# Mixer of block 1: weights rounded first in each step, attention outputs copied out of PSUM, statistic and gate rows and the second output turn later

## The reference

```python
h = rmsnorm(x, mix_norm_pre[l])
z = h @ w_in[l]
aq, ak, av, mq, mk, mv, mo, mi, mf, gl = jnp.split(z, SPLIT_IDX, axis=-1)
ya = diff_attention(aq, ak, av, lam, lam_init, attn_norm_w[l])   # 8 heads
mqk = jax.nn.silu(causal_depthwise_conv(jnp.concatenate([mq, mk], axis=-1), conv_w[l], conv_b[l]))
hm = mlstm_chunkwise(...mqk..., mv, mi + igate_b[l], mf + fgate_b[l])
ym = (jax.nn.sigmoid(mo) * rmsnorm(hm, mlstm_norm_w[l]).reshape(b_, s_, M_V))
g_a, g_m = jnp.split(jax.nn.sigmoid(gl + gate_b[l]), 2, axis=-1)
merged = g_a * (ya @ w_proj_a[l]) + g_m * (ym @ w_proj_m[l])
x = x + rmsnorm(merged @ w_out[l], mix_norm_post[l])
```

## Time and profile before

| | us |
|---|---|
| Runs, median (lowest to highest of 3) | 2140.96 (2139.83 to 2142.47) |
| The profiled execution | 2136.9 |
| Its span, first to last instruction | 2135.1 |
| TensorE busy | 2005.8 |
| VectorE busy | 1342.9 |
| ScalarE busy | 1077.9 |
| Mean granted TensorE clock, share of full | 0.973 |

### The profile page before, as it was taken

The page is one execution under the profiler, slowest core; times in us unless marked ns, Lnnn a source line. Parts: engine busy times, 40 slices in busy tenths (PEclk is TensorE's granted clock), DMA queues, the critical chain, the costliest instruction groups (busy, mean ns, idle before and its releaser), DMA issues. The chain is left out here.

```text
span 2135.1 us, 31214 instructions
## 1 busy us (share of the span) xinstructions
PE 2005.8 (94%) x12360; PEld 1768.7 (83%) x12360; DVE 1342.9 (63%) x2263; ACT 1077.9 (50%) x1669; POOL 228.1 (11%) x212
## 2 busy tenths in 40 slices
PE   7999978999999999989799999997989998999997
PEld 5887778899788778878789978876889997789997
DVE  6555667466755565566756675557578865668874
ACT  5445456564544554455564554444355545346553
POOL 1000301000100000011100010002104400303420
PEclk9999999999999999999999999997999999899998
DMA  7554434535555365544354455553235563334552
GB/s 255 188 188 156 139 101 143 169 126 183 191 191 188 120 215 188 188 138 129 103 184 135 155 188 189 190 168 102 86 118 188 180 216 117 99 119 154 182 194 73
DMA packets 92737, 338.30 MB, mean 158 GB/s; under 512 B 10288, under 2 KB 10544, under 8 KB 92592
## 3 DMA queue, kind: packets, MB, share of 16 engines
q1 hardware_dynamic: 91296, 330.69, 46.6%
q0 software_dynamic: 720, 4.69, 0.6%
q10 hardware_dynamic: 576, 0.92, 0.1%
HBM read 335.21 MB, written 1.05 MB: 157 GB/s over the span
## 5 line engine op out<-in xcount | busy, mean ns | idle before, releaser
L983 DVE TENSOR_TENSOR w_lo<-w_raw,w_hi 128x1024 fp32r<-128x1024 f32 x628 | 790.1, 1263 | 479.6 <-ACT w_hi L534 477.4
L534 ACT ACTIVATE w_hi<-w_raw 128x1024 fp32r<-128x1024 f32 x628 | 658.9, 1054 | 432.3 <-PE stream L1746 197.1
L1738 PE MATMUL stream<-h_hi,w_hi 128*128 128x256 f32 x1632 | 480.7, 295 | 12.1 <-DVE h_lo L1357 9.6
L1739 PE MATMUL stream<-h_lo,w_hi 128*128 128x256 f32 x1632 | 467.5, 286 | 0.0
L1740 PE MATMUL stream<-h_hi,w_lo 128*128 128x256 f32 x1632 | 467.3, 286 | 0.0
L1738 PEld LDWEIGHTS stream<-h_hi,w_hi 128*128 128x128 f32 x1632 | 317.1, 194 | 25.4 <-issue 18.1
L1744 PE MATMUL stream<-w_hi,h_hi 128*128 128x512 f32 x800 | 314.6, 393 | 6.1 <-DVE h_lo L996 6.1
L1739 PEld LDWEIGHTS stream<-h_lo,w_hi 128*128 128x128 f32 x1632 | 318.1, 195 | 0.2
L1740 PEld LDWEIGHTS stream<-h_hi,w_lo 128*128 128x128 f32 x1632 | 317.7, 195 | 0.0
L1746 PE MATMUL stream<-w_lo,h_hi 128*128 128x512 f32 x800 | 313.1, 391 | 0.0
L1745 PE MATMUL stream<-w_hi,h_lo 128*128 128x512 f32 x800 | 312.9, 391 | 0.0
(11 more groups left out here) (309 smaller groups left out, 2981.0 us busy)
## 6 DMA issues: line engine op xcount, KB each, us to landing
w_raw<-in_w_up SPq DMA_DIRECT2D x264, 512.0 KB, 3.5
w_raw<-in_w_mix SPq DMA_DIRECT2D x228, 512.0 KB, 3.5
w_raw<-in_w_down SPq DMA_DIRECT2D x136, 512.0 KB, 3.5
params<-in_params POOLq DMA_DIRECT2D x4, 921.5 KB, 5.2
out_x<-x_residual SPq DMA_DIRECT2D x4, 256.0 KB, 2.3
constants<-in_consts POOLq DMA_DIRECT2D x1, 896.0 KB, 7.8
x_residual<-in_x ACTq DMA_DIRECT2D x3, 256.0 KB, 4.1
x_residual<-in_x SPq DMA_DIRECT2D x1, 256.0 KB, 3.9
```

The costliest lines, as they stand in the source:

```text
L534: nc.scalar.activation(w_hi[:, u % RING], w_raw[:, u % RAW], ACT.Copy).then_inc(hi_ready, 1)
L983: nc.vector.tensor_tensor(w_lo[:, u % RING], w_raw[:, u % RAW], w_hi[:, u % RING].bitcast(F32), ALU.subtract).then_inc(split_done, 1)
L1738: nc.tensor.matmul(dst, w_hi[:, s, w], hi, start=first, stop=False)
L1739: nc.tensor.matmul(dst, w_hi[:, s, w], lo, start=False, stop=False)
```

## The change

- In each step, ScalarE calls `hi_next()` first; before, it stood behind the exponentials, the transposed weights' copy, the squares and the roundings of the outputs. Eight roundings and splits instead of five stand ahead of the statistics, and none between the v copies.
- `o_square` becomes `o_take`: ScalarE copies both PSUM tiles into `o_n` (SBUF) and squares from there. The values of head 4, and the first mLSTM values that reuse the tiles, wait for these copies; `o_scale` works on `o_n` in place. The wait for the turns that still read `o_n` goes from VectorE to ScalarE.
- Statistic rows move from within unit 5 to step 8, gate rows from within unit 6 to step 10; the ScalarE and VectorE work on them moves to steps 10 and 11, the maxima to steps 16 to 23, the split of the rows to step 25.
- The second pair of output turns moves from steps 32, 33 to 35, 37 on all three engines; on ScalarE `ya_round` now stands ahead of the exponentials of its step.
- The sigmoids of `gl` start at step 65.

```diff
@@ -447,6 +447,7 @@
         tok_bank = ((bank[0], bank[1]), (side[0], side[1]), (bank[2], bank[0]), (bank[1], bank[2]),
                     (bank[0], bank[1]), (bank[2], bank[0]))
         GROUPS = ((0, 3), (3, 6), (6, 8))
+        YA_TURN = (25, 27, 35, 37)
         YM_TURN = (57, 63, 65, 68)
 
         def out_bank(i):
@@ -667,10 +668,15 @@
                         act.wait_ge(o_ready, n8 + h)
                     nc.scalar.activation(aT[:], bank[3][:, 0:3 * P], ACT.Copy).then_inc(aT_stored, 1)
 
-                def o_square(b):
+                def o_take(b):
                     act.wait_ge(o_ready, n8 + 4 * b + 4)
+                    if b > 0:
+                        act.wait_ge(ya_turned, l * 4 + 2)
                     for t in range(QT):
-                        nc.scalar.activation(o_sq[:, t], side[2 + t][:], ACT.Square).then_inc(o_squared, 1)
+                        nc.scalar.activation(o_n[:, t], side[2 + t][:], ACT.Copy).then_inc(o_squared, 1)
+                    for t in range(QT):
+                        act.wait_ge(o_squared, (l * 2 + b) * 4 + 2)
+                        nc.scalar.activation(o_sq[:, t], o_n[:, t], ACT.Square).then_inc(o_squared, 1)
 
                 def o_rstds(b):
                     act.wait_ge(o_stat, (l * 2 + b) * 5 + 4)
@@ -725,7 +731,7 @@
                         nc.scalar.activation(yms_hi[:, 2 * p + j], bank[3][:, j * T:(j + 1) * T], ACT.Identity,
                                              scale=p1("mlstm_norm", 2 * p + j)).then_inc(ym_hi_done, 1)
 
-                for j in range(5):
+                for j in range(8):
                     hi_next()
                 act.wait_ge(pre_stat, n + 1)
                 nc.scalar.activation(ln_all[:], bank[3][:, 0:T + QT], ACT.Ln, bias=eps1[:]).then_inc(pre_ln, 1)
@@ -733,25 +739,24 @@
                 nc.scalar.activation(rs_all[:], ln_all[:], ACT.Exp, scale=-0.5).then_inc(pre_rs, 1)
                 act.wait_ge(pre_rs, n + 1)
                 store(0, lambda t: av_tok[:, t, 0:512])
-                hi_next()
-                hi_next()
-                lam_exponents()
-                hi_next()
                 store(1, lambda t: av_tok[:, t, 512:D])
                 for i in range(U_QK, U_OUT):
-                    if i == U_QK + 1:
+                    hi_next()
+                    if i == U_QK + 2:
+                        lam_exponents()
+                    if i == U_QK + 3:
                         gates()
+                    if i in YA_TURN:
+                        k = YA_TURN.index(i)
+                        ya_round(k // 2, k % 2)
                     if i % 2 and 11 <= i <= 25:
                         attn_exp((i - 11) // 2)
                     if i % 2 == 0 and 14 <= i <= 28:
                         attn_turned((i - 14) // 2)
                     if i in (21, 29):
-                        o_square((i - 21) // 8)
+                        o_take((i - 21) // 8)
                     if i in (22, 30):
                         o_rstds((i - 22) // 8)
-                    if i in (25, 27, 32, 33):
-                        k = (25, 27, 32, 33).index(i)
-                        ya_round(k // 2, k % 2)
                     if i == 34:
                         nc.scalar.preload_act_table_set("silu_and_others")
                         act.wait_ge(conv_done, (l + 1) * 8)
@@ -791,8 +795,8 @@
                             mlstm_rstd(g)
                     if i in YM_TURN:
                         ym_round(YM_TURN.index(i))
-                    if 66 <= i < 70:
-                        for m in range(4 * (i - 66), 4 * (i - 65)):
+                    if 65 <= i < 69:
+                        for m in range(4 * (i - 65), 4 * (i - 64)):
                             act.wait_ge(gl_scaled, l * 16 + m + 1)
                             nc.scalar.activation(gl[:, m], gl[:, m], ACT.Sigmoid,
                                                  bias=p1("gate_b", m)).then_inc(gl_sig, 1)
@@ -1174,7 +1178,7 @@
                     k = (l * 2 + b) * 5
                     dve.wait_ge(p_ready, n8 + 4 * b + 4)
                     nc.vector.reciprocal(o_r0[:], aden[:, 4 * b:4 * b + 4, 0:2])
-                    dve.wait_ge(o_squared, (l * 2 + b) * 2 + 2)
+                    dve.wait_ge(o_squared, (l * 2 + b) * 4 + 4)
                     for t in range(QT):
                         nc.vector.tensor_reduce(o_var[:, :, t], o_sq[:, t].rearrange("p (h d) -> p h d", h=4), AX.X,
                                                 ALU.add).then_inc(o_stat, 1)
@@ -1188,11 +1192,9 @@
                     dve.wait_ge(o_rstd, l * 2 + b + 1)
                     nc.vector.tensor_tensor(o_r0[:], o_r0[:], o_rs[:], ALU.mult).then_inc(o_stat, 1)
                     dve.wait_ge(o_stat, k + 5)
-                    if b > 0:
-                        dve.wait_ge(ya_turned, l * 4 + 2)
                     for t in range(QT):
                         nc.vector.tensor_tensor(o_n[:, t].rearrange("p (h d) -> p h d", h=4),
-                                                side[2 + t][:].rearrange("p (h d) -> p h d", h=4),
+                                                o_n[:, t].rearrange("p (h d) -> p h d", h=4),
                                                 o_r0[:, :, t].unsqueeze(2).to_broadcast([P, 4, P]),
                                                 ALU.mult).then_inc(o_scaled, 1)
 
@@ -1284,29 +1286,27 @@
                                                 ALU.subtract).then_inc(mix_lo, 1)
 
                 prepare()
-                for j in range(5):
+                for j in range(8):
                     lo_next()
                 dve.wait_ge(pre_rs, n + 1)
                 scales()
-                lo_next()
-                lo_next()
-                rows()
-                lo_next()
                 for i in range(U_QK, U_OUT):
+                    if i == U_QK + 2:
+                        rows()
                     if i % 2 and 11 <= i <= 25:
                         attn_mask((i - 11) // 2)
                     if i % 2 == 0 and 12 <= i <= 26:
                         attn_combine((i - 12) // 2)
                     if i in (22, 30):
                         o_stats((i - 22) // 8)
-                    if 14 <= i < 22:
-                        gate_max(i - 14)
-                    if i == 23:
+                    if 16 <= i < 24:
+                        gate_max(i - 16)
+                    if i == 25:
                         split_rows()
                     if i == 31:
                         g_tok()
-                    if i in (25, 27, 32, 33):
-                        k = (25, 27, 32, 33).index(i)
+                    if i in YA_TURN:
+                        k = YA_TURN.index(i)
                         ya_rest(k // 2, k % 2)
                     lo_next()
                     if i in (22, 30):
@@ -1945,7 +1945,7 @@
                 def values(h):
                     pe.wait_ge(aT_stored, n8 + h + 1)
                     if h == 4:
-                        pe.wait_ge(o_scaled, l * 4 + 2)
+                        pe.wait_ge(o_squared, l * 8 + 2)
                     v, c = av_tok[:, :, h * P:(h + 1) * P], blk(h % 4)
                     nc.tensor.matmul(side[2][:, c], aT[:, 0:P], v[:, 0], start=True, stop=True)
                     nc.tensor.matmul(side[3][:, c], aT[:, P:T], v[:, 0], start=True, stop=False)
@@ -1988,7 +1988,7 @@
                             if g == 0:
                                 pe.wait_ge(tok_stored, l * 12 + 12)
                                 pe.wait_ge(nm_cleared, l + 1)
-                                pe.wait_ge(o_scaled, l * 4 + 4)
+                                pe.wait_ge(o_squared, l * 8 + 6)
                             else:
                                 pe.wait_ge(num_taken, (l * 3 + g) * 2)
                             first = a
@@ -2049,21 +2049,21 @@
                         chunk(0, j, t)
                 for j in range(4):
                     unit(u0 + 4 + j)
-                    chunk(1, j, 0)
-                    if j == 1:
+                    for t in range(QT):
+                        chunk(1, j, t)
+                for i in range(U_QK, U_OUT):
+                    if i == U_QK:
                         stat_rows()
-                    chunk(1, j, 1)
-                    if j == 2:
+                    if i == U_QK + 2:
                         gates()
-                for i in range(U_QK, U_OUT):
                     if i % 2 and 11 <= i <= 25:
                         scores((i - 11) // 2)
                     if i % 2 == 0 and 14 <= i <= 28:
                         turn_a((i - 14) // 2)
                     if i % 2 and 15 <= i <= 29:
                         values((i - 15) // 2)
-                    if i in (25, 27, 32, 33):
-                        k = (25, 27, 32, 33).index(i)
+                    if i in YA_TURN:
+                        k = YA_TURN.index(i)
                         ya_turn(k // 2, k % 2)
                     if i == 31:
                         g_tok()
```

## The result

| | before | after |
|---|---|---|
| Runs beside each other, median us (lowest to highest, 4 each) | 2141.72 (2139.83 to 2142.92) | 2085.93 (2084.01 to 2088.39) |
| The profiled execution, us | 2136.9 | 2084.01 |
| Its span, us | 2135.1 | 2082.2 |
| Mean granted TensorE clock | 0.973 | 0.979 |

The ratio is 0.9741, 95% interval 0.9724 to 0.9758: 55.8 us less, 2.6%. The forecast was 2097, so 44 us less, and its range began at 2091; the time lies 5 us under it. The direction was right, and the waits that were to go are gone, but for a rest of 1.0 us. The size was 9 us of span too small, and the prices that the single parts were given did not hold, as the experiments show.

A forecast was written before the change was run, and what follows sets the result against it. TensorE, busy 94%, was taken as the bound, leaving only its stalls and half clock: 41.1 us of waits plus 6.95 for clock is 48.0, less 4 is 44.0, so 2140.96 falls to 2097 us; 8-in-10 range 2091 to 2108.

The forecast's parts named there:

- Weights first: Attention steps of both mixers: rounding ahead of the exponentials makes k copies timely, ending score waits of 9.0 + 3.6 = 12.6 us.
- Outputs leave PSUM at once: Fifth head's values, both mixers: they wait only for two ScalarE copies, not the scaled outputs; 12.1 us gained, added costs taken as 0.
- Statistic rows later: Start of both mixers: rows moved behind more token units no longer wait for GpSimd's sum; 4.4 us gained.
- Second turn later, ya_lo and the merge: Later mixer steps: waits for gate columns (6.8 us), ya_lo (3.8 us) and the gated merge (1.4 us) go.
- The half clock: Four stretches behind stalls in the mixers: 13.9 us of TensorE work at clock 0.50 takes twice as long, costing 6.95 us.
- What comes late next: Steps 22 to 33: VectorE falls 4.0 us behind per layer, split lead absorbs part; 2 us per layer allowed, 4 us off.
- the ceiling of 48.0 us: Both mixers of block 1: all winnable time, 41.1 us of waits plus 6.95 for the clock; set the range's lower end.
- VectorE as the bound (2105): Rival, steps 22 to 33: VectorE's 4.0 us lag per layer is not absorbed; gain 36.0 us, 2105 us; 18%.
- the q copy (2109.5): Rival, attention scores: they wait for ScalarE's q copy, not k, so 12.6 us stay; gain 31.4, 2109.5 us; 8%.
- the slower case (2215): Rival, steps 8 to 63: rounding first delays ScalarE results TensorE needs at once, 1.05 us each, 118 us, 2215 us; 3%.

The follow-up runs named there:

- the experiment with the k copy: Kernel before, with VectorE's k copy ahead of the split in odd steps and ScalarE untouched: 2132.41 us against 2134.16, ratio 0.9988.
- the loaded kernel: Kernel after, with VectorE repeating its split in six steps of each mixer, 12 extra splits: 2100.78 us against 2133.9 for the kernel before, ratio 0.9834.

## Why the prediction was right, and where its size was off

**Weights first**, 12.6 us: right in mechanism. The split follows the maxima, the k copy is in time, and the chain ends at k and not q, as the experiment with the k copy shows. The gain in this stretch is 13.4. But as a price of the part 12.6 is far too low: alone it gives 31 us. The single terms were attached to the wrong owners. That their sum still comes near is luck of a kind: all parts were made together, so it didn't matter which of them a wait belonged to.

**Outputs leave PSUM at once**, 12.1 us: 12.3 measured with the other parts there. Alone it loses 6 us, and taken out it costs only 7, wait and clock together. The costs that I set to 0 by their cover, in the tile view (duration min/median/max, ns):

```profile
L676 ACT ACTIVATE o_normed<-acc x8: 572/582/602, 290.6 to 1007.7; 128x512 f32<-128x512 f32 x8
L679 ACT ACTIVATE o_squares<-o_normed x8: 614/624/634, 291.6 to 1008.9; 128x512 f32<-128x512 f32 x8
```

The copies take 0.58 us (0.6 assumed), the squares from SBUF 0.62 and so 0.10 more than from PSUM, the upper end of my 0 to 0.8 us in all. The second scaling runs beside GpSimd:

```profile
326.62 1.85 DVE L1196 TENSOR_TENSOR o_normed<-o_normed,o_row_scales 128x512 f32<-128x512 f32 x2
```

The first one, in the timeline above, took 1.29 us, this one 1.85: 0.56 more a layer, near the upper end of 0.7. Of its two instructions the first takes the usual 0.69 us and the second 1.24. GpSimd's own instruction beside it is longer as well, 1.14 us against 0.77 for the same one 4.6 us earlier:

```profile
322.14 0.77 POOL L1628 TENSOR_TENSOR conv_in<-conv_raw,mix_rstd 128x256 f32<-128x256 f32 x1 [3.12 <-ACT conv_raw L782]
326.79 1.14 POOL L1628 TENSOR_TENSOR conv_in<-conv_raw,mix_rstd 128x256 f32<-128x256 f32 x1 [3.87 <-ACT conv_raw L782]
```

So the engine that comes second loses each time, as the rule of the Trainium skill, SBUF — State Buffer, section "SBUF: two separate sides", would have it: GpSimd's instruction starts 0.17 us into the first scaling and is stretched, and the second scaling starts inside it and is stretched in turn. The size is about that of the convolution rows. Both costs are real, and none of these reached TensorE.

**Statistic rows later**, 4.4 us and 1.2 of clock: 6.0 measured, 5.6 in layer 0 and 0.4 in layer 1. The rows start at 235.18 with nothing to wait for; I had 235.4. Layer 0 gave 1.9 us beyond its wait and not 1.2: the clock was low in the rows themselves too (0.64 from 232.20 to 233.60 of before), and the prediction's window began behind them. Of the new wait for the v tokens' copy I had said 0.6 us of cover; 0.4 us of waiting in layer 1 shows that there was none there. The gate rows' "no cost" held only because the rounding first had given VectorE room: with this part alone, GpSimd's scan fell on VectorE's work and made the third scores 1.7 us later.

**Second turn later, ya_lo and the merge**: gate columns 9.1 with the clock, against 8.5; one ya_lo wait a layer stays, 0.5 us, at

```profile
314.38 0.52 PE L1942 MATMUL stream<-constants,attn_scores 128*128 128x128 f32 x3 [0.48 <-DVE ya_lo L1203]
```

The merge gave 1.19 us in each layer and not 0.70. In the trace of before, the first matmul behind that wait starts 0.98 us behind the one ahead of it, where the usual distance is 0.12: the wait cost 0.86, not the 0.70 of its row. Of the remaining 0.33 us some 0.25 stand at the last turn of the mLSTM outputs, which started 0.35 us behind the matmul ahead of it at 474.77 before, and 0.12 behind it after.

**The half clock**, 13.9 / 2: "twice as long" was too much. At 0.50 TensorE's matmuls of 256 columns start 0.213 us apart and at 1.00 0.120, so 1.8 times. Behind the values the clock gave 2.1 us in layer 0 and 1.4 in layer 1, 3.6 where 4.05 stood.

**The step that failed is "What comes late next"**: the 4 us taken off for VectorE. The waits left are 1.4 us in place of 4, so 2.6 of the 8.9 us of error. I had compared 44.91 us of VectorE work with 40.9 us of TensorE in one window of before. But those 44.91 held work that VectorE had been kept from until then (its split of the step before started at 304.49), and at the window's end it had run ahead during TensorE's stalls. The same TensorE work after holds 38.79 us of VectorE's, in 86 instructions and not 96, against 39.92 of TensorE's: two splits fewer, one at each end. (What the change itself moved across the window's ends, ya_lo out and maxima in, is 1.5 us each way.) So it fell behind by next to nothing there. My reason for allowing only half, that the lead of splits absorbs a lag, was wrong too: in the loaded kernel 8.1 us of work cost 7.3 and 8.0 us. Two errors, one of which was about the demand and one about the cover. By itself this step would have left the time inside the range; what put it outside is the ceiling of 48.0 us (below, at the range).

The other 6.3 us of the span's error are in the main three omissions. First, each wait that goes takes some hundredths more with it than its idle row says: the six score waits of a layer are 6.3 us in their rows and gave 6.68, so 0.06 each; over 22 waits, and with 0.16 for each of the two merges, that is about 1.6 us. Second, a wait of 0.3 us for ya_lo at the second turn had a line of its own, which I left out. Third, 2.9 us lie outside the mixers: the stretches of low clock between the layers fall elsewhere or not at all. I had no row that would have told me where they fall. Some 1.5 us are left: 0.7 at the merge, 0.2 net from the two corrections of the clock, and 0.6 that I can't place.

The median adds 2.2 us. I had put the 4.1 us between median and profiled execution on top again; after, it is 1.9. With the 9 us between 2093 and 2084.0 this makes the 11 us between 2097 and 2086.

Of the rivals, VectorE as the bound (2105) did not happen, though the loaded kernel shows how near it was; the q copy (2109.5) is refuted by an experiment of its own; the slower case (2215) has no trace in any run: nothing waits for a result that the rounding has been put in front of.

**The range** was wrong at its lower end. It was set at "all 48.0 us won", as if the idle rows and the half clock that I could see were a ceiling. They weren't: the mixers alone gave 50.0, and 2.9 us came from outside. With 48.0 us the median would have been 2093; the measured one is 7 us lower, 2.0 of them from the mixers, 2.9 from outside and 2.2 from the distance between median and profiled execution. The 2 us allowed for the spread of the runs didn't cover that.

## What to carry to other kernels

Waits that one cross-engine loop feeds are not a list of prices. Before adding their rows, ask for each which queue the releaser stood in, and put all that stand in one queue down to what holds that queue up; here one moved line gave 31 of the 56 us, and all other parts without it 0.35%. Where an operation is needed in the same step, a lead elsewhere in the queue is no cover. And the busy time of a window belongs to that window only if the engine entered and left it in step: compare its instruction count, not just its microseconds.

## What the runs showed that I had not expected

GpSimd's sum ahead of the statistic rows in layer 0 takes one of three durations, in kernels that don't differ in it. Before, after, and the kernel with the second turn alone:

```profile
222.62 9.54 POOL L1594 TENSOR_TENSOR h<-h 128x1024 f32<-128x1024 f32 x3 [202.97 <-ACT h L547]
```

```profile
222.62 10.65 POOL L1594 TENSOR_TENSOR h<-h 128x1024 f32<-128x1024 f32 x3 [203.48 <-ACT h L548]
```

```profile
220.96 7.01 POOL L1594 TENSOR_TENSOR h<-h 128x1024 f32<-128x1024 f32 x3 [201.43 <-ACT h L547]
```

9.54, 10.65 and 7.01 us for the same three instructions; in the fourteen profiled executions of this case it is 7.0 in seven, 9.5 to 9.6 in five and 10.6 in two, and in layer 1 always 6.5. With 7.0 TensorE waits 1.2 us for it where the rows stand at their old place, with 9.5 the 3.7 us of the earlier trace rows. So a part of what moving the rows gains is insurance: after, TensorE doesn't wait even for 10.65.

The traces show what sets the duration: whether GpSimd or VectorE gets in first. VectorE and the middle instruction of the sum, before and then with the second turn alone:

```profile
222.72 2.37 DVE L1093 TENSOR_TENSOR attn_norm_scaled<-params 128x1 f32<-128x1 f32 x1
...
225.62 4.61 DVE L983 TENSOR_TENSOR w_lo<-w_raw,w_hi 128x1024 fp32r<-128x1024 f32 x4
...
L1594 POOL TENSOR_TENSOR h<-h 128x512 f32<-128x512 f32 x1 | 6.2, 6206 | 0.1
```

```profile
221.05 0.15 DVE L1093 TENSOR_TENSOR attn_norm_scaled<-params 128x1 f32<-128x1 f32 x1
...
221.86 9.46 DVE L983 TENSOR_TENSOR w_lo<-w_raw,w_hi 128x1024 fp32r<-128x1024 f32 x5
...
L1594 POOL TENSOR_TENSOR h<-h 128x512 f32<-128x512 f32 x1 | 2.2, 2154 | 0.1
```

In the long case GpSimd is in first, and VectorE's small instruction stands for 2.37 us. Then four splits follow each other at their usual 1.2 us, and GpSimd's middle instruction lasts 6.2 us, over all four. In the short case VectorE has that small one behind it, and from then on split and sum alternate, the splits stretched up to 3.3 us and the middle instruction done in 2.2. The 9.5 and the 10.6 us differ in the last instruction, 0.7 or 1.8 us: it is long where VectorE's next split started just ahead of it. All seven short and all seven long executions follow this pattern. So a difference of some 0.1 us at the start decides over 2.5 us of the sum, and with the wait and the clock over 4.2 us of the kernel before.

And half clock comes and goes with the waits: behind waits of 2.2 us there were 3.4 us at 0.50, behind those of 6.1 us 4.8 and 3.3, and with the waits gone the same places run at 1.00. In the trace of after no window behind the remaining waits of the mixers is below 1.00. The length of the wait alone doesn't tell: with the rounding first alone, waits of 1.9 us in the same place were followed by 1.00 in layer 0 and 0.64 in layer 1.
